# Delta rule's entry: eight extra float32 sums on TensorE, and the gates' products one quarter later

## The chip, the cores and the metric

The kernel runs on one core of a Trainium2 chip, in one launch. The metric is the device time of one execution in microseconds (us). Before the change it is 851.34 us, the median of three runs (849.03 to 851.57). Lower is better.

## The reference

Two transformer blocks in float32 over 256 tokens of width 1024. The first has windowed attention with an mLSTM, cross attention and a gated feed-forward part. The second has a gated delta rule layer and a stick-breaking attention layer. The change lies at the entry of the delta rule:

```python
proj = h @ w_in                                     # q, k, v, z and two gate columns for each of 8 heads
qkv = silu(causal_conv(proj[..., :3 * W], conv_w))  # 4 taps
q = _l2norm(q) * Dh ** -0.5
k = _l2norm(k)                                      # _l2norm: x * rsqrt(sum(x * x) + EPS)
beta = sigmoid(b_raw)
g = -exp(a_log) * softplus(a_raw + dt_bias)         # the gates
o = _chunk_gated_delta(q, k, v, g, beta)            # chunks of 64 tokens, 8 heads of 128
o = _rms(o, o_gain) * silu(z)
y = o @ w_out
```

## The kernel before

Activations lie transposed in on-chip memory, 8 tiles of 128 channels by 256 tokens. Each weight matrix is cut into units of 1024 rows by 256 columns (1 MB). SyncE's queue loads them in a fixed order into five raw buffers. ScalarE (line 1121) writes the rounded high half of a unit and VectorE (line 1522) the low half, in four pieces. A unit is then four "parts" (quarters) on TensorE, each with three products for each of two row blocks: high by high, low activation by high weight, high activation by low weight (line 2047, 12 matmuls in a quarter, 48 in a unit; in this stage the low weight comes last).

A planner in Python (`class Plan`) writes one list of jobs, and each engine carries out its own jobs in the order of that list and waits on counting semaphores. So the list fixes the order on every engine. `step()` adds the next quarter of the weight stream, with pieces of later units' high and low halves ahead of it. `blend()` runs generators beside it: in each round every active generator goes on to its next `yield`, and then one step of the stream is added. A `yield` is so worth a quarter.

In the delta rule's stage two generators are active at a time, first `gdn_gates` and `gdn(0)`:

- `gdn_gates`: g_mm, 32 float32 matmul instructions of 32 columns of weights for the two gates (line 2106), reads the normed activations that ScalarE's job `xa` finishes (line 1179). g_cp copies them (VectorE, line 1732), g_tp adds the four row groups up (TensorE, line 2115). g_abs is exponential and logarithm (ScalarE, lines 1310 to 1317), g_neg, g_a and g_m are VectorE's (lines 1752 to 1772), g_ctp transposes (TensorE, lines 2125 to 2128), then g_col, g_exp and g_c3 (lines 1778, 1322, 1781).
- `gdn(i)`, for a pair of heads: it begins when the SiLU of its pair (`gsilu`, line 1108) and g_c3 stand in the list. d_sq squares q and k (ScalarE, line 1413); d_ones sums over the 128 channels with a matrix of ones (TensorE, line 2246, two float32 matmuls of 512 columns, two instructions each); d_rs is logarithm and exponential (ScalarE, lines 1419 and 1422, behind a table load, line 1100). Then come d_nrm (VectorE, line 1858), d_vtp (line 2252), d_vb (line 1866), d_dec (lines 2261 to 2264, waits for the second d_rs), d_dexp (line 1433), d_ktp (line 2270), d_kt (line 1875), d_kk (line 2278) and the inverse of a triangular matrix in six levels.

The weight stream beside it is unit qkva 0, 4, 8, 1, 5, 9, and so on; the convolution's taps are `gid` (ScalarE, line 1268) and `gtap` (VectorE, line 1519, three instructions for each half of a unit). g_mm stands ahead of the first quarter of qkva 4, g_cp ahead of the second, g_tp, g_abs and g_a ahead of the third, g_m ahead of the fourth; g_ctp and g_col ahead of the third quarter of qkva 8, g_exp and g_c3 ahead of its fourth. d_ones 0 stands behind the third quarter of qkva 1. A `gtap` half stands ahead of each of the first two quarters of a unit. Two older places in the kernel have products that nobody reads: line 2005 at the start, and the job `busy` (line 2073).

Of the kernel before, what the change touches and what calls it, by code (L numbers as in the profile page):

```python
# [14 lines left out]
T = 256  # L15
# [191 lines left out]
class Plan:  # L207
# [23 lines left out]
    def add(self, kind, *i):  # L231
        self.jobs.append((kind, *i))
        self.done.add((kind, *i))
# [159 lines left out]
    def make(self):  # L393
        add = self.add
# [231 lines left out]
        self.handler["za"] = lambda i: add("za", i)  # L626

        def gdn_gates():
            for _ in range(4):
                yield  # L630
            add("g_mm", 2)
            yield
            add("g_cp", 2)
            yield
            add("g_tp", 2)
            add("g_abs", 2)
            add("g_neg")
            add("g_a", 2)
            yield
            add("g_m", 2)  # L640
            for _ in range(3):
                yield
            add("g_ctp", 2)
            add("g_col", 2)
            yield
            add("g_exp")
            add("g_c3")

        def gdn(i):
            while ("gsilu", i) not in self.done or ("g_c3",) not in self.done:  # L650
                yield
            for n in range(2):
                add("d_sq", i, n)
            yield
            for n in range(2):
                add("d_ones", i, n)
                add("d_rs", i, n)
            yield
            for n in range(2):
                add("d_nrm", i, n)  # L660
            add("d_vtp", i)
            add("d_vb", i)
            add("d_dec", i, 0)
            add("d_dexp", i, 0)
            yield
            add("d_dec", i, 1)
            add("d_dexp", i, 1)
            yield
            add("d_ktp", i)
            add("d_kt", i)  # L670
            for n in range(2):
                add("d_kk", i, n)
                add("d_am", i, n)
            add("d_u0", i)
            yield
            add("d_utp", i)
            add("d_t0", i)
            for lev in range(1, 7):
                yield
                add("d_x", i, lev)  # L680
                add("d_xm", i, lev)
                yield
                add("d_uu", i, lev)
                add("d_u", i, lev)
            yield
            add("d_v0", i)
            add("d_v0c", i)
            yield
            add("d_s", i)
            add("d_sc", i)  # L690
            add("d_qd", i)
            add("d_qexp", i)
            add("d_qs", i)
            yield
            add("d_ks", i)
            add("d_vb1", i)
            yield
            add("d_v1", i)
            add("d_v1c", i)
            yield  # L700
            add("d_o", i)
            add("d_osq", i)
            yield
            if i == 3:

                add("d_oz", i)
                for n in range(2):
                    add("d_oones", i, n)
                    add("d_ors", i, n)
                    add("d_on", i, n)  # L710
                yield
                for n in range(2):
                    add("d_ohi", i, n)
                    add("d_olo", i, n)
                return
            add("d_oones", i)
            add("d_ors", i)
            yield
            add("d_on", i)
            while ("za", i) not in self.done:  # L720
                yield "park"
            add("d_oz", i)
            yield "park"
            while ("za!", 3) not in self.done or (i and ("d_ohi", i - 1) not in self.done):
                yield "park"
            add("d_ohi", i)
            yield "park"
            add("d_olo", i)

        self.handler["outa"] = residual("outa", "kv")  # L730
        add("f_m", "kv")
        self.blend([gdn_gates()] + [gdn(i) for i in range(4)], 2, self.at("sbk"))
        self.run_to(self.at("sbk"))
        self.flush_lows()
# [100 lines left out]
def program(nc, xT, memT, cB, vec, con, conr, wg1, wg2, wst, wsd, outT):  # L835
# [11 lines left out]
    with ctx:  # L847
        def sb(name, shape, dt=F32, c=ctx):
            return c.enter_context(nc.sbuf_tensor(name, shape, dt))
# [10 lines left out]
        def on(*job):  # L860
            return S[COUNTED[job[0]]], rank[job]

        def tick(kind):
            return S[COUNTED[kind]], 1
# [15 lines left out]
        ps = [ctx.enter_context(nc.psum_tensor(f"ps{i}", [P, 512], F32))[:, :] for i in range(3)]  # L880
# [6 lines left out]
        cst = sb("cst", [P, NCON])  # L887
# [63 lines left out]
        def C(name, a=0, b=None, p=P):  # L951
            a0, n = CON[name]
            return cst[0:p, a0 + a:a0 + (n if b is None else b)]
# [5 lines left out]
        ident, ones = C("ident"), C("ones")  # L959
# [1033 lines left out]
        def _(t):  # L1993
            e = Once(t)
# [11 lines left out]
            for kind, *i in jobs:  # L2006
                if kind == "part":
                    k, part = i
                    name, n, kc, w = units[k]
                    hi, lo, _ = IN[name]  # L2010
# [20 lines left out]
                    for half in turns:  # L2031
                        a, b = hi if half[0] == "h" else lo, wh if half[1] == "h" else wl
                        for c in chunks:
# [12 lines left out]
                            for q, (o, l, r) in enumerate(ops):  # L2046
                                ins = t.matmul(o, l, r, start=begins and k0 == 0 and half == "hh" and c == 0 and q == 0,  # L2047
                                               stop=ends and not more and half == turns[2] and c == kc - 1 and q == len(ops) - 1,
# [19 lines left out]
                elif kind == "busy":  # L2068

                    name, count = i  # L2070
# [16 lines left out]
                elif kind == "f_ones":  # L2087
# [3 lines left out]
                             stop=True).then_inc(*tick("f_ones"))  # L2091
                elif kind == "f_s1":
                    t.matmul(ps[4][:, 0:T], ones, tr[5][:, 0:T], start=False, stop=True).then_inc(*tick("f_s1"))
                elif kind == "g_mm":
# [7 lines left out]
                    for c in range(KC):  # L2102
                        r = slice(32 * (c % 4), 32 * (c % 4) + 32)
                        for half in range(2):
                            o = (2 * c + half) * n
                            ins = t.matmul(ps[5][r, half * T:(half + 1) * T], g[:, o:o + 32], tmp[:, c, :], start=c < 4 and half == 0,
                                           stop=c >= 4 and half == 1, skip_group_check=True)
# [97 lines left out]
                elif kind == "c_qk":  # L2205
# [6 lines left out]
                    for b in range(2):  # L2212
                        for c in range(2):
                            ins = t.matmul(bank[:, b * T:(b + 1) * T], xq[:, 2 * h + c, b * P:(b + 1) * P], xk[:, 2 * h + c, :],  # L2214
                                           start=c == 0, stop=c == 1)
# [12 lines left out]
                elif kind == "c_av":  # L2228
# [5 lines left out]
                    for c in range(2):  # L2234
                        cc = slice(h * T + c * P, h * T + (c + 1) * P)
                        for m in range(2):
                            ins = t.matmul(ps[4 + 2 * slot][:, c * T:(c + 1) * T], xvv[:, m, cc], pt[:, m * T:(m + 1) * T], start=m == 0, stop=m == 1)  # L2237
                    ins.then_inc(*tick("c_av"))
                elif kind == "d_ones":
                    n_, n = i  # L2240
                    e.wait_ge(*on("d_sq", n_, n))
# [39 lines left out]
                elif kind == "d_utp":  # L2281
                    n_, = i
                    e.wait_ge(*on("d_u0", n_))
                    for h in range(2):
                        for c in range(2):
                            for k in range(2):
                                src = HALVES[k ^ c]
                                ins = t.matmul(xb[n_ % 2][HALVES[k], c, h, :], Uc[n_ % 2][src, c, h, :], ident[src, src],
                                               start=True, stop=True)
# [12 lines left out]
                elif kind == "d_uu":  # L2302
# [3 lines left out]
                    for h in range(2):  # L2306
                        for c in range(2):
                            if lev == 6:
                                ins = t.matmul(ub[n_ % 2][0:64, c, h, :], X_[64:128, c, h, :], Um[n_ % 2][64:128, 2 * h + c, 64:128],
                                               start=True, stop=True)  # L2310
# [24 lines left out]
                elif kind == "d_qd":  # L2335
                    n_, = i
                    for n in range(2):
                        h = 2 * n_ + n
                        ins = t.matmul(ps[4 + 2 * (n_ % 2)][:, n * P:(n + 1) * P], C("ident", h, h + 1, p=8).broadcast_to([8, P]), R2[:, P:T],
                                       start=True, stop=True)  # L2340
# [7 lines left out]
                elif kind == "d_v1":  # L2348
# [3 lines left out]
                    for n in range(2):  # L2352
                        ins = t.matmul(ps[4 + 2 * (n_ % 2)][:, n * P:(n + 1) * P], Um[n_ % 2][:, 2 * n + 1, :], vb[:, 2 * (2 * n_ + n) + 1, :],
                                       start=True, stop=True)
# [151 lines left out]
```

## Time and profile before

| | us |
|---|---|
| median of three runs | 851.34 |
| lowest, highest | 849.03, 851.57 |
| the profiled execution | 849.51 |
| its span, first to last instruction | 847.7 |
| TensorE, VectorE, ScalarE busy in the span | 804.3, 639.5, 494.7 |

The profiled execution is one execution; its mean granted clock of TensorE is 0.994 of full speed. In the rows below a row of an engine's order of time is one run of like instructions: its start, how long it lasted, the line of the kernel and the operands (written tile first). A number in brackets is the time the engine stood idle ahead of it, with the work that ended the wait. TensorE's instructions overlap, so that the steps between starts give the rate and the last one's end is modelled. PE is TensorE, PEld its weight loads (which overlap), DVE VectorE, ACT ScalarE, POOL GpSimd. In the windows the first number behind the stretch is its length, (xN) counts instructions, and a clock of 1.00 is 2.4 GHz, 0.50 is 1.2 GHz.

### The profile page before, as it was taken

What the parts mean: (1) busy time and instruction counts of PE and PEld (TensorE: products, weight loads), DVE (VectorE), ACT (ScalarE), POOL (GpSimd) and SP (SyncE); (2) the same over time, 40 slices, a digit from 0 to 9 for tenths busy, and PEclk for the clock granted to TensorE, in tenths of its full rate; (3) what the DMA queues carried; (4) which work ended last, traced back from release to release, by engine and by line L of the source; (5) the groups of instructions that cost most, each with busy time, mean ns of one, the idle gap of its engine ahead of it and who ended that gap; (6) DMA issues with size and microseconds to landing.
All of it is one profiled execution on the core that took longest, in us unless ns stands there. A gap on an engine that the chain in (4) does not pass through costs nothing.

```text
span 847.7 us, 16950 instructions
## 1 busy us (share of the span) xinstructions
PE 804.3 (95%) x7092; PEld 744.7 (88%) x7092; DVE 639.5 (75%) x1288; ACT 494.7 (58%) x1016; POOL 0.2 (0%) x4
## 2 busy tenths in 40 slices
PE   7999999999999999999998798999999899999988
PEld 5888889999999999999996687888888889978888
DVE  5488988897687899978888777877867778954455
ACT  5578655454456666665547646373756455667762
POOL 0000000000000000000000000000000000000000
PEclk9999999999999999999999899999999999999999
DMA  9632674875455566646793322221324248744211
GB/s 358 240 122 104 237 261 149 288 259 199 158 196 194 193 226 232 230 152 217 272 335 133 100 100 101 101 101 51 116 98 160 82 150 293 293 155 149 100 51 51
DMA packets 22541, 148.52 MB, mean 175 GB/s; under 512 B 2624, under 2 KB 3264, under 8 KB 6336
## 3 DMA queue, kind: packets, MB, share of 16 engines
q1 hardware_dynamic: 22464, 147.43, 49.2%
q8 instruction: 56, 0.92, 0.4%
q14 instruction: 21, 0.17, 0.1%
HBM read 146.37 MB, written 1.05 MB: 174 GB/s over the span
## 4 chain that ended last, share of the span: by engine, by line
PE 72%; DVE 18%; ACT 9%; issue 1%; ACTq 0%; DVEq 0%
PE ps L2047 52%; DVE wlo L1522 4%; DVE raw L1544 3%; DVE tmp L1519 1%; PE pp L2299 1%; PE pp L2319 1%; PE pp L2278 1%; PE pp L2246 1%; PE pp L2237 1%; DVE vt L1519 1%; PE pp L2214 1%; ACT whi L1121 1%; PE pp L2314 1%; PE ps L2005 1%; PE pp L2403 1%
## 5 line engine op out<-in xcount | busy, mean ns | idle before, releaser
L1522 DVE TENSOR_TENSOR wlo<-raw,whi 128x512 fp32r<-128x512 f32 (+2 forms) x436 | 273.8, 659 | 17.0 <-ACT whi L1121 16.6
L1121 ACT ACTIVATE whi<-raw 128x512 fp32r<-128x512 f32 (+2 forms) x436 | 239.1, 600 | 0.0
L2047 PE MATMUL ps<-p0hi,whi 128*128 128x256 f32 x1128 | 192.9, 292 | 6.3 <-ACT p0hi L1173 5.3
L2047 PE MATMUL ps<-p0hi,wlo 128*128 128x256 f32 x1128 | 180.8, 281 | 4.7 <-DVE wlo L1522 4.4
L2047 PE MATMUL ps<-p0lo,whi 128*128 128x256 f32 x1128 | 180.8, 281 | 1.1 <-DVE p0lo L1522 0.9
L2047 PEld LDWEIGHTS ps<-p0hi,whi 128*128 128x128 f32 x1128 | 154.1, 189 | 20.9 <-issue 12.3
L2047 PEld LDWEIGHTS ps<-p0hi,wlo 128*128 128x128 f32 x1128 | 152.9, 189 | 6.6 <-DVE wlo L1522 6.6
L2047 PEld LDWEIGHTS ps<-p0lo,whi 128*128 128x128 f32 x1128 | 153.3, 189 | 2.0 <-DVE p0lo L1522 1.7
L1544 DVE CUSTOM_DVE_ANT_0 raw<-raw,cact,vc 128x1024 f32<-128x1024 f32 x64 | 81.7, 1277 | 0.0
L2047 PE MATMUL ps<-zhi,wlo 128*128 128x256 f32 x176 | 31.1, 280 | 0.6 <-DVE wlo L1522 0.6
L1137 ACT ACTIVATE tr<-x 128x512 f32<-128x512 f32 (+1 forms) x18 | 10.3, 584 | 35.6 <-DVE x L1678 24.1
L2047 PE MATMUL ps<-zhi,whi 128*128 128x256 f32 x176 | 31.0, 279 | 0.0
L2047 PE MATMUL ps<-zlo,whi 128*128 128x256 f32 x176 | 30.8, 278 | 0.0
L1519 DVE SCALAR_TENSOR_TENSOR tr<-pp,tr 128x384 f32<-128x384 f32 x20 | 11.1, 557 | 25.0 <-ACT tr L1502 24.4
L1100 ACT ACT_TABLE_LOAD x22 | 28.2, 1283 | 1.1 <-PEq L2499 0.7
L1693 DVE TENSOR_TENSOR tr<-ps,rs 128x512 f32<-128x512 f32 x22 | 15.1, 688 | 16.5 <-PE ps L2047 16.5
L1228 ACT ACTIVATE tr<-tr,vc 128x256 f32<-128x256 f32 x22 | 13.3, 602 | 22.8 <-DVE tr L1693 22.8
L2047 PEld LDWEIGHTS ps<-zhi,wlo 128*128 128x128 f32 x176 | 25.0, 188 | 1.2 <-DVE wlo L1522 1.2
L2047 PEld LDWEIGHTS ps<-zhi,whi 128*128 128x128 f32 x176 | 25.1, 188 | 0.1
L2047 PEld LDWEIGHTS ps<-zlo,whi 128*128 128x128 f32 x176 | 25.0, 188 | 0.0
L1519 DVE SCALAR_TENSOR_TENSOR Tm<-pp,Tm 128x512 f32<-128x512 f32 (+1 forms) x20 | 12.7, 635 | 13.6 <-PE pp L2319 13.6
L2047 PE MATMUL ps<-q1hi,whi 128*128 128x256 f32 x128 | 21.6, 290 | 0.5 <-ACT q1hi L1170 0.4
(353 smaller groups left out, 1245.3 us busy)
## 6 DMA issues: line engine op xcount, KB each, us to landing
raw<-wst SPq DMA_DIRECT2D x125, 1024.0 KB, 5.0
raw<-wsd SPq DMA_DIRECT2D x16, 704.0 KB, 4.6
x<-xT SPq DMA_DIRECT2D x2, 512.0 KB, 4.6
m_x<-memT SPq DMA_DIRECT2D x1, 1024.0 KB, 8.9
outT<-x SPq DMA_DIRECT2D x3, 256.0 KB, 2.3
cact<-cB SPq DMA_DIRECT2D x1, 512.0 KB, 13.8
cst<-con SPq DMA_DIRECT2D x1, 356.0 KB, 11.8
smo<-conr SPq DMA_DIRECT2D x1, 320.0 KB, 11.4
```

The source lines that it names most:

```text
L1100: act.preload_act_table_set(name)
L1121: act.activation(whi[n % NHL][:, a:b], raw[k % NRAW][:, a:b], ACT.Copy).then_inc(*tick("hi"))
L1137: act.activation(dst, src, ACT.Square).then_inc(*tick("sq"))
L1228: act.activation(tr[c % 3][:, 0:T], tr[3 + c % 3][:, 0:T], ACT.Identity, scale=V("cff_w", c * 3 + 2), bias=V("cff_b", c)).then_inc(*tick(" ...
L1519: return v.scalar_tensor_tensor(out=out, in0=a, scalar=s, in1=b, op0=op0, op1=op1)
L1522: return v.tensor_tensor(lo, src, hi.bitcast(F32), ALU.subtract)
L1544: v.tensor_tensor_reduce(out=r, in0=r, in1=cact[:, :], scale=1.0, scalar=V(bname, 2 * n + m), op0=ALU.mult, op1=ALU.add, accum_out=mod[:, ...
L1693: v.tensor_tensor(tr[3 + c % 3].rearrange("p (m t) -> p m t", m=2), bank_of("up", c).rearrange("p (m t) -> p m t", m=2), rep(rs[:, :], 2), ...
L2005: t.matmul(stats[:, 0:T], tr[3][:, 0:P], tr[3][:, 0:T], start=True, stop=True)
L2047: ins = t.matmul(o, l, r, start=begins and k0 == 0 and half == "hh" and c == 0 and q == 0, stop=ends and not more and half == turns[2] and ...
L2214: ins = t.matmul(bank[:, b * T:(b + 1) * T], xq[:, 2 * h + c, b * P:(b + 1) * P], xk[:, 2 * h + c, :], start=c == 0, stop=c == 1)
L2237: ins = t.matmul(ps[4 + 2 * slot][:, c * T:(c + 1) * T], xvv[:, m, cc], pt[:, m * T:(m + 1) * T], start=m == 0, stop=m == 1)
```

## The change

The generator `gdn_gates` waits five rounds rather than four before g_mm, so that all its jobs stand one quarter later in the list. In `gdn(0)` alone a job `d_busy` of eight stands between the squares and d_ones. On TensorE it waits for g_c3 (which d_ones 0 waits for too) and issues eight float32 matmuls of the matrix of ones with 256 columns of the constants into bank ps[3], which d_ones then overwrites. Nobody reads them. In the new list the quarter of qkva 4 that stood behind g_mm stands ahead of it; g_cp stands behind the second `gtap` half of qkva 0; g_m stands behind `gid` 4; g_ctp is ahead of the fourth quarter of qkva 8 and g_exp, g_c3 behind `gid` 8. The other jobs keep their order.

```diff
--- before.py
+++ after.py
@@ -626,7 +626,7 @@
         self.handler["za"] = lambda i: add("za", i)
 
         def gdn_gates():
-            for _ in range(4):
+            for _ in range(5):
                 yield
             add("g_mm", 2)
             yield
@@ -652,6 +652,8 @@
             for n in range(2):
                 add("d_sq", i, n)
             yield
+            if i == 0:
+                add("d_busy", 8)
             for n in range(2):
                 add("d_ones", i, n)
                 add("d_rs", i, n)
@@ -2236,6 +2238,12 @@
                         for m in range(2):
                             ins = t.matmul(ps[4 + 2 * slot][:, c * T:(c + 1) * T], xvv[:, m, cc], pt[:, m * T:(m + 1) * T], start=m == 0, stop=m == 1)
                     ins.then_inc(*tick("c_av"))
+                elif kind == "d_busy":
+
+                    count, = i
+                    e.wait_ge(*on("g_c3"))
+                    for _ in range(count):
+                        t.matmul(ps[3][:, 0:T], ones, cst[:, 0:T], start=True, stop=True)
                 elif kind == "d_ones":
                     n_, n = i
                     e.wait_ge(*on("d_sq", n_, n))
```

## Rows read from the trace of the kernel before

**Rows 1.** The page, busy time and share of TensorE.

```profile
PE 804.3 (95%) x7092; PEld 744.7 (88%) x7092; DVE 639.5 (75%) x1288; ACT 494.7 (58%) x1016; POOL 0.2 (0%) x4
```

**Rows 2.** Windows: busy PE, PEld, DVE, ACT, POOL, then clock, DMA share, GB/s.

```profile
457.00:458.00 1.00, 0.00 (x0) 0.00 (x0) 1.00 (x4) 1.00 (x4) 0.00 (x0) 1.00 0.00 0
...
481.00:482.00 1.00, 0.00 (x0) 0.00 (x0) 0.94 (x2) 0.62 (x2) 0.00 (x0) 0.93 0.93 393
...
488.00:489.00 1.00, 1.00 (x7) 1.00 (x7) 0.17 (x2) 0.97 (x3) 0.00 (x0) 0.66 0.00 0
...
490.00:495.00 5.00, 5.00 (x31) 3.95 (x30) 4.85 (x12) 2.88 (x11) 0.00 (x0) 1.00 0.43 138
...
673.00:676.00 3.00, 2.81 (x13) 2.52 (x13) 2.89 (x8) 2.42 (x5) 0.00 (x0) 0.50 0.00 0
```

**Rows 3.** TensorE in order of time: start, us, line, operands, [idle before, releaser].

```profile
458.83 1.98 PE L2106 MATMUL pp<-tmp,g 128*32 128x256 f32 x32 [2.18 <-ACT tmp L1179]
...
460.74 0.74 PE L2047 MATMUL ps<-p0hi,whi 128*128 128x256 f32 x4
...
463.91 1.02 PE L2115 MATMUL pp<-tr,cst 128*8 128x512 f32 x2
...
471.33 0.22 PE L2125 MATMUL pp<-cst,rows 8*128 8x8 f32 x1 [0.55 <-DVE rows L1772]
...
471.79 0.74 PE L2047 MATMUL ps<-p0hi,whi 128*128 128x256 f32 x4
...
478.44 0.63 PE L2047 MATMUL ps<-p0hi,wlo 128*128 128x256 f32 x4
...
483.76 3.78 PE L2246 MATMUL pp<-tr,cst 128*128 128x512 f32 x4 [4.69 <-ACT tr L1413]
...
486.55 1.84 PE L2047 MATMUL ps<-p0hi,whi 128*128 128x256 f32 x4
...
489.72 0.36 PE L2261 MATMUL pp<-crt 128*128 128x256 f32 x1
```

**Rows 4.** Chain of waits that ended last: start, us, engine, line.

```profile
483.08 0.64 ACT tr L1413
```

**Rows 5.** VectorE in order of time, 459 to 497 us.

```profile
459.33 2.50 DVE L1522 TENSOR_TENSOR wlo<-raw,whi 128x512 fp32r<-128x512 f32 x4 [0.62 <-ACT whi L1121]
...
463.17 0.68 DVE L1732 COPY tr<-pp 128x512 f32<-128x512 f32 x1
...
463.77 0.68 DVE L1522 TENSOR_TENSOR wlo<-raw,whi 128x512 fp32r<-128x512 f32 x1
...
464.37 1.51 DVE L1519 SCALAR_TENSOR_TENSOR qT<-ps,vc,qT 128x255 f32<-128x255 f32 x3
...
467.24 0.14 DVE L1752 TENSOR_SCALAR sm<-sm 8x1 f32<-8x1 f32 x1 [1.36 <-ACT rows L1317]
...
468.48 0.67 DVE L1522 TENSOR_TENSOR wlo<-raw,whi 128x512 fp32r<-128x512 f32 x1
...
496.02 0.61 DVE L1875 TENSOR_SCALAR tmp<-pp,cols 128x128 f32<-128x128 f32 x2 [0.85 <-PE pp L2270]
```

**Rows 6.** TensorE in order of time, three other places.

```profile
1.18 6.78 PE L2005 MATMUL ps<-tr 128*128 128x256 f32 x16 [1.18 <-DVE tr L1524]
...
448.22 1.46 PE L2073 MATMUL ps<-cst 128*128 128x256 f32 x6
...
672.81 1.08 PE L2047 MATMUL ps<-p0hi,wlo 128*128 128x256 f32 x4 [1.80 <-DVE wlo L1522]
```

**Rows 7.** ScalarE in order of time, 484 to 489 us.

```profile
484.76 1.28 ACT L1100 ACT_TABLE_LOAD   x1
...
486.06 0.69 ACT L1419 ACTIVATE tr<-pp,cst 128x512 f32<-128x512 f32 x1
...
487.58 0.69 ACT L1419 ACTIVATE tr<-pp,cst 128x512 f32<-128x512 f32 x1 [0.17 <-PE pp L2246]
...
488.30 0.63 ACT L1422 ACTIVATE tr<-tr 128x512 f32<-128x512 f32 x1
```

## Prediction

> **What bounds the kernel now.** I read the page first: TensorE is busy for 95% of the span [rows 1]. A stage that leaves TensorE idle is therefore worth a look, and the windows show one. In the microsecond from 481 TensorE does nothing and its granted clock begins to fall from full speed to half (2.4 to 1.2 GHz); it comes back only in the one from 488 [rows 2]. TensorE's own order of time shows why: a quarter of weight unit qkva 1 ends at 479.07, and the first pair's sums of squares (d_ones, line 2246) start at 483.76 after 4.69 us of waiting for ScalarE's squares (line 1413). These four instructions and the next quarter then run at half clock [rows 3].
>
> What releases the squares is read from the chain of waits and VectorE's order. Squares (483.08) wait for the SiLU, the SiLU for the taps of unit qkva 8 (the values' convolution), and VectorE works through taps and low halves almost without a pause from 467.24 to 481.3. It stands idle once ahead of that, 1.36 us before line 1752, for ScalarE's gate work, which came from the gate's selection product g_tp, which came from the copy g_cp [rows 4, 5]. So in this stage VectorE's order bounds the entry of the delta rule, and the gates' chain lies on it. From 490 on TensorE is full again [rows 2].
>
> **The eight sums.** `d_busy` puts eight float32 products of 128x256 on TensorE behind its wait for g_c3, each two instructions. The nearest rows: six such instructions of line 2073 take 1.46 us at full clock, 0.216 us apart, and sixteen of line 2005 take 6.78 us at half clock at the start of the kernel [rows 6]. Sixteen at full clock are 15 x 0.216 + 0.38 = 3.6 us; that and 6.8 are the two bounds. I take 3.6, since TensorE has worked at full clock up to them. They fit in the wait (4.69 now, 5.4 after the shift below), so they cost nothing; the cover fails only if TensorE reaches them less than 3.6 us before the squares land. g_c3 is done before 477 now and some 2 us later after the change, still ahead of them, and nothing behind the added wait starves, because d_ones waits for the same g_c3.
>
> **What a full clock is worth there.** TensorE would win most of 2 us: the quarter behind d_ones would end at about 485.5 + 1.4 rather than 489.3 (486.55 and some 2.7 us at half clock) [rows 3]. But the next product that matters, d_dec (line 2261, at 489.72), waits for the second inverse root, and that is ScalarE's: squares, one high half, a table load of 1.28 us ending at 486.04, then logarithm and exponential twice, ending at 488.93. The first logarithm starts when the table is there, not when the sums are; the second waits 0.17 us for the cold sums [rows 7]. With warm sums the second root ends at 488.76, so d_dec could start at 488.8: a gain of 0.9 us, not 2. The bounds of this gain are 0 (clock falls all the same) and 0.9.
>
> **The gates a quarter later.** This moves g_mm (32 instructions) behind the first quarter of unit qkva 4, and with it g_cp, g_tp, g_abs, g_a, g_m, g_ctp, g_col, g_exp and g_c3 each behind one more quarter of PE, one more high half of ScalarE, and one or two more pieces of VectorE. No DMA is issued with them; SP's and POOL's queues are not passed, but the low halves that free raw buffers shift with VectorE.
> - TensorE waits for `xa` now: 2.18 us, until 458.83. After the change a quarter stands there, which needs the high half of qkva 4; ScalarE makes that right behind `xa`, and it is ready when VectorE's first low half starts, 459.33 [rows 3, 5]. The wait is not filled: 0.5 us longer. A quarter is 1.42 us (14 steps from 471.79 to 478.44, 0.475 each, three to a quarter) and g_mm 1.91 (458.83 to 460.74): first quarter 459.3 to 460.7, g_mm to 462.6, second quarter to 464.1, third to 465.5.
> - VectorE: the copy g_cp starts at 463.17 now, ahead of a low half (0.60) and the second taps (1.42) [rows 5]. After, both come first: g_cp starts at 465.2 and lands 0.74 later (463.17 to g_tp's 463.91), g_tp at 465.95, 2.04 us later than now. TensorE is there at 465.5, so VectorE decides.
> - From g_tp to line 1752 it is 3.33 us (463.91 to 467.24) [rows 3, 5], so line 1752 moves to 469.28. Of the 2.04 us VectorE fills 0.60 with the low half that it does at 468.48 now, the first of those behind g_a. Its idle time grows from 1.36 to 2.8 us: **VectorE is 1.43 us later** from there on. It makes taps and low halves without slack up to the SiLU, so SiLU, squares and d_ones move from 483.76 to 485.2.
> - g_m ends at 473.4 rather than 471.3; TensorE reaches g_ctp at 466.9 + 4 x 1.42 = 472.6 and waits 0.8 there (0.55 now), then some 0.3 for a low half. It gets to d_busy at about 479.8, the sums end at 483.4, and 1.8 us of waiting are left before d_ones at 485.2.
>
> The bounds of this part: 1.43 if nothing absorbs it, and 0 if the taps of this stage were not what the squares wait for, for which no row speaks.
>
> **The sum.** d_dec starts when the second root is there: 488.93 - 0.17 + 1.43 = 490.2, against 489.72 now. That is +0.5 us. Its other waits are shorter. VectorE is 0.9 us later behind its second norm product, but stands idle 0.85 us before d_kt at 496.02 [rows 5], which takes that up; TensorE is full through 490 to 495 [rows 2] and carries 0.5 on, as each engine's order behind it is unchanged. The profiled execution would go from 849.51 (span 847.7 and 1.8 around it) to 850.0. It lies 1.83 under the median of the three runs, 851.34; on that median the sum gives **851.8**.
>
> **A rule on the clock.** The clock doesn't fall at every gap of the size that is left. It stayed full over the 2.18 us before 458.83, and fell after 1.80 us before 672.81, where TensorE then ran at half clock through 673 to 676 [rows 2, 3, 6]. So length alone doesn't decide, and 1.8 us is no safe gap. The Trainium skill, "TensorE: Matmul & The Clock Gate", What's actually happening, says that the monitor's windows run freely and don't start with the kernel; by that rule such a gap is cold in some executions and not in others, here and at 672.81. The trace agrees as far as its two gaps go. By it the sum would be 0.5 in some executions and about 1.4 in others.
>
> **The rivals.**
> 1. *The sums don't keep the clock*: it falls in the 1.8 us that are left. For it: 672.81. Against: 458.83. Then the stage runs as now, 1.43 later: 851.34 + 1.4 = 852.8.
> 2. *Slower than now*: a fall comes late in that gap, so that the cold stretch reaches past d_dec, where TensorE is full. Its price beyond rival 1 is a further stretch like that at 673: 3 us and a part of the next one at half speed, some 1.6 us of TensorE's work [rows 2]. In all 1.43 + 1.6 = 3.0: 854.4. It decides from the point where the half clock still holds at d_dec, 491. Against it: now the stretch ends at 488.3, ahead of d_dec.
> 3. *VectorE's delay is absorbed*, because the gates' chain doesn't move the taps as I read it, and the gain of the clock stands alone: -0.9, 850.4. For it: only that idle times in a trace are inferred. Against it: the 1.36 us before line 1752.
> 4. *The clock elsewhere*, by the rule named above: the stretch at 673 isn't cold. Its 3 us at half clock cost 1.5 us of TensorE's work [rows 2], so 1.5 less: with my sum -1.0 (850.3), with rival 3 -2.4 (848.9).
>
> **How the numbers follow.** My forecast 0.58, rival 1 0.14, rival 2 0.06, rival 3 0.11, rival 4 0.11. All but one lie within 2.5 us of the median, which is the 0.3% that a measurement of this kernel can tell (the three runs alone differ by 2.5). Faster by more than 0.3% is half of rival 4 and a rest: 0.08. Slower is rival 2 and a rest: 0.07. Within 0.3%: 0.85. The range reaches from rival 4's far end (848.9) to rival 1 and half of the step to rival 2: 853.6.
>
> **What would show it.** In the changed kernel's trace: sixteen instructions of the new line end about 1.8 us before d_ones; the granted clock from 481 to 490 is 1.00; g_tp starts near 466, VectorE's idle time before the line that scales -exp(alog) by -1 is 2.8 us rather than 1.4; d_ones near 485.2; the first logarithm follows the table load and not the sums; d_dec near 490.2. The prediction is wrong if g_tp isn't later than 465, if d_ones stays at 483.8, if d_dec comes 1 us or more before 490, or if the sums run at half clock and hold d_ones up.

## The result: slower by half a percent, with the forecast entry intact

The changed kernel takes 854.81 us, the median of 20 executions; the kernel before takes 850.94 in the same 20 turns. The ratio is 1.0052 with a 95% interval of 1.0037 to 1.0066. I had forecast 851.8 and a range up to 853.6, so this is **slower, and above the range**. The single times say more than the median: those of before lie between 849.03 and 852.52, those of the changed kernel between 850.52 and 859.9. Eight of the 20 are over 855. Each execution comes with a mean granted clock of TensorE; it goes from 0.996 in the fastest down to 0.984 in the slowest.

The profiled execution (850.96 us, span 849.2) is one of the quick ones. TensorE's order of time in it, lines 2246 (new) and 2254 (d_ones) among them, columns as in [rows 3]:

```profile
460.12 0.73 PE L2049 MATMUL ps<-p0hi,whi 128*128 128x256 f32 x4 [2.66 <-ACT whi L1123]
...
461.72 1.97 PE L2108 MATMUL pp<-tmp,g 128*32 128x256 f32 x32
...
466.71 1.02 PE L2117 MATMUL pp<-tr,cst 128*8 128x512 f32 x2
...
480.76 3.62 PE L2246 MATMUL pp<-cst 128*128 128x256 f32 x16
485.96 1.98 PE L2254 MATMUL pp<-tr,cst 128*128 128x512 f32 x4 [1.58 <-ACT tr L1415]
...
489.75 0.63 PE L2260 MATMUL pp<-cst,vt 128*128 128x128 f32 x4 [0.41 <-ACT tr L1424]
490.90 0.38 PE L2269 MATMUL pp<-crt 128*128 128x256 f32 x1 [0.52 <-ACT tr L1424]
```

and VectorE's, first low half of the stage and the line that scales -exp(alog), then ScalarE's second load and roots:

```profile
460.10 2.50 DVE L1524 TENSOR_TENSOR wlo<-raw,whi 128x512 fp32r<-128x512 f32 x4 [0.62 <-ACT whi L1123]
...
470.05 0.14 DVE L1754 TENSOR_SCALAR sm<-sm 8x1 f32<-8x1 f32 x1 [2.79 <-ACT rows L1319]
```

```profile
486.96 1.28 ACT L1102 ACT_TABLE_LOAD   x1
488.26 0.69 ACT L1421 ACTIVATE tr<-pp,cst 128x512 f32<-128x512 f32 x1
```

The reader should first subtract 0.77 us: the stage begins that much later (460.10 against 459.33 in [rows 5]). It is lost far ahead of the change: VectorE loses 0.3 us between 20 and 30 us, behind a stretch of TensorE at half clock from 12 to 19, and 0.58 between 405 and 410, where every other profile of this document is later than that of before by the same 0.58. Then every step of the sum is there. g_tp comes 2.03 us later (466.71 against 463.91 in [rows 3]; forecast 2.04). VectorE's idle time is 2.79 (forecast 2.8). d_ones comes at 485.19 on the old scale (forecast 485.2), 1.58 us behind the sums (forecast 1.8), at full clock. The first logarithm follows the table load as in [rows 7]. d_dec comes at 490.13 (forecast 490.2, now 489.72), and the first product of the triangular stage 0.42 us later than before (501.92 less 0.77, against 500.73 in the trace of before). So this quick execution is what the sum described, and the loss must be in the others. The rows with 0.41 and 0.52 in brackets are two waits that the kernel before doesn't have there: it reached both places late and found its operands ready.

### The profile page after: what moved, and what is told of

Its sections match the earlier page's. It is cut to its first block, busy times and chain, and to the rows that moved or that the text cites. A ratio compares the mean times of both kernels' runs of the same rounds, so it can differ in the third digit from the quotient of the medians.

```text
span 849.2 us, 16981 instructions
## 1 busy us (share of the span) xinstructions
PE 807.7 (95%) x7108; PEld 748.8 (88%) x7108; DVE 639.6 (75%) x1288; ACT 494.6 (58%) x1016; POOL 0.2 (0%) x4
## 4 chain that ended last, share of the span: by engine, by line
PE 72%; DVE 17%; ACT 9%; issue 1%; DMA 1%; SPq 0%; ACTq 0%; DVEq 0%
PE ps L2049 54%; DVE wlo L1524 4%; DVE raw L1546 3%; DVE tmp L1521 1%; PE pp L2307 1%; PE pp L2327 1%; PE pp L2286 1%; ACT whi L1123 1%; PE pp L2239 1%; DVE vt L1521 1%; PE pp L2216 1%; PE pp L2322 1%; PE pp L2411 1%; PE pp L2422 1%; DVE kT L1521 1%
## 5 line engine op out<-in xcount | busy, mean ns | idle before, releaser
L1139 ACT ACTIVATE tr<-x 128x512 f32<-128x512 f32 (+1 forms) x18 | 10.2, 583 | 35.6 <-DVE x L1680 24.1
```

Of the source, the lines that this page charges most:

```text
L1139: act.activation(dst, src, ACT.Square).then_inc(*tick("sq"))
```

## Experiments

For each run the time is the median (lowest and highest in brackets), and the ratio is to the executions of the kernel before in the same turns, with its 95% interval. "Sums" are float32 products of a matrix of ones with 256 columns, which nobody reads; each is two instructions. A job `fill` of n issues n of them into a bank that is free there (`stats`, ps[7]); the code cuts show only where it stands in the list, not the lines that issue it. "The wait for `xa`" is TensorE's long wait ahead of g_mm, which with the later gates ends with the high half of qkva 4.

### The changed kernel again

No edit.

> The changed kernel again, for a second profile and its spread. Known: its 20 executions lie between 850.5 and 859.9 with mean granted clocks from 0.984 to 0.996, those of before between 849.0 and 852.5. Theory P (phase): with the certain fall of the clock at the entry gone, the clock's later or earlier changes fall differently in each execution, and a slow execution shows one or more half-clock stretches of about 6.8 us that the profiled one of 850.96 (half clock at 12 to 19 and 674 to 678) doesn't have, anywhere behind 480 us. Theory L (local): a slow execution shows the half clock at the entry itself, from the 1.6 us gap before d_ones on, and nowhere else; then no execution can be over 1.4 + 1.6 above before. P expects a ratio of 1.003 to 1.007 and single executions over 855; L at most 1.0035.

Measured: 856.57 us (852.02 to 857.38), ratio 1.0049 (1.0034 to 1.0064), 8 of 12 executions over 855. Its profiled execution took 857.38, and its windows show the loss:

```profile
491.00:492.00 1.00, 0.96 (x4) 0.77 (x5) 0.98 (x3) 1.00 (x3) 0.00 (x0) 1.00 0.00 0
492.00:493.00 1.00, 1.00 (x7) 0.66 (x6) 1.00 (x4) 0.60 (x3) 0.00 (x0) 0.99 0.06 16
493.00:494.00 1.00, 1.00 (x7) 1.00 (x6) 0.96 (x3) 1.00 (x5) 0.00 (x0) 0.50 0.00 0
...
502.00:503.00 1.00, 1.00 (x7) 1.00 (x7) 0.44 (x1) 0.00 (x0) 0.00 (x0) 0.50 0.00 0
503.00:504.00 1.00, 1.00 (x9) 1.00 (x9) 0.41 (x2) 0.00 (x0) 0.00 (x0) 0.89 0.00 0
```

The granted clock (third number from the right) falls at the very end of the microsecond from 492 and stays at half for 10.2 us in all, with TensorE busy all the time. A second stretch of 3.4 us, from 533.9 to 537.3, lies behind the second pair's d_dec, which waits 0.52 us ahead of it, as it does in the kernel before. In TensorE's order of time it reads so:

```profile
489.89 0.63 PE L2260 MATMUL pp<-cst,vt 128*128 128x128 f32 x4 [0.41 <-ACT tr L1424]
491.04 0.39 PE L2269 MATMUL pp<-crt 128*128 128x256 f32 x1 [0.52 <-ACT tr L1424]
...
493.19 1.05 PE L2049 MATMUL ps<-p0lo,whi 128*128 128x256 f32 x4
...
506.69 0.46 PE L2296 MATMUL pp<-cst,Tm 64*64 64x64 f32 x16 [1.47 <-DVE Tm L1899]
```

From d_ones (486.10) to the first 64x64 product it is 20.59 us, against 16.97 in the trace of before (483.76 to 500.73) and 15.96 in the changed kernel's first profile (485.96 to 501.92): 4.6 us lost behind an entry that had won one. Theory L is out: the fall isn't at the gap before d_ones. Theory P has its stretch behind 480.

### Each part alone

Against the kernel before:

```diff
-            for _ in range(4):
+            for _ in range(5):
                 yield
             add("g_mm", 2)
```

> Only the gates a quarter later; no eight sums. The wait before d_ones is then some 5.3 us, and the clock must fall there as before. Theory P: the fall is certain, so the executions lie as close together as those of before (within 4 us), and their median is 1.4 us above before (1.0017). Rival G (the gates' order is what costs, through later waits of VectorE and TensorE): the spread up to 859 and a ratio of 1.005 are here too, without the sums.

Measured: 853.94 us (851.03 to 856.92), ratio 1.0033 (1.0018 to 1.0047). Both were wrong in part: more than my 1.43, less than all. The profile shows the clock low from 461 to 465, behind the wait ahead of the first quarter of qkva 4:

```profile
458.00:461.00 3.00, 1.03 (x8) 1.04 (x9) 2.37 (x7) 3.00 (x8) 0.00 (x0) 1.00 0.00 0
461.00:464.00 3.00, 3.00 (x30) 1.69 (x32) 2.93 (x7) 2.75 (x6) 0.00 (x0) 0.55 0.18 27
```

From g_mm to g_tp it takes 6.31 us there, 4.99 in the changed kernel's first profile. At the entry it has the old stretch at half clock (6.8 us, from 485.2 to 492.0), and d_dec follows d_ones by 5.85 us, 5.96 in the kernel before: nothing more is lost there.

The other part alone is the changed kernel with `range(4)` again.

> Only the eight sums; gates where they were. 3.6 of the 4.7 us are filled, about 1.1 us of waiting is left. The step of my sum: d_dec 0.9 us earlier, ratio 0.999. Theory P: the fall isn't certain any more, so executions with added half-clock stretches are seen (over 855) and the ratio is 1.002 to 1.006, although the entry itself is shorter. Rival G: ratio 0.999 and executions within 4 us.

Measured: 852.17 us (849.14 to 854.19), ratio 1.0005 (0.9992 to 1.0018). Theory P missed here: no execution over 855, and no loss that can be told. My 0.9 us of gain isn't in the median, but it is in the profile (852.63 us): d_dec follows d_ones by 4.94 us, 5.96 in the kernel before. Two other stretches at half clock hide it there. One of 3.4 us begins at 459.9, behind the old wait of 2.18 us, which [rows 3] shows and [rows 2] shows without a fall: from g_mm to g_tp it takes 6.52 us, 5.08 before. The other, near 675, lasts 6.8 us where the kernel before has 3.4. The two short waits of 0.41 and 0.52 are the same as in the changed kernel, but the clock didn't fall behind them.

### The changed kernel a third time

No edit, one execution.

> The changed kernel a third time, one look: one more draw of where the half-clock stretches lie. Theory P: the entry at full clock, and zero to two stretches of 3.4 or 6.8 us elsewhere behind 480. Theory L: none but at the entry, at about 674 and in the first 20 us.

Measured: 854.51 us. The clock fell at 492 to 496 (3.4 us), and from d_ones to the first 64x64 product it was 17.47 us, 1.5 more than without a fall. So a fall at this place comes with different lengths. The larger part of this execution's excess lies elsewhere: near 677 its half clock lasts 6.8 us rather than 3.4, and VectorE loses 2.3 us between 670 and 700 against the kernel before.

```profile
677.00:683.00 6.00, 4.80 (x22) 4.64 (x22) 4.28 (x8) 2.91 (x6) 0.00 (x0) 0.50 0.41 135
```

### Filling the two short waits, and the long one before d_ones

Against the changed kernel:

```diff
+            if i == 0:
+                add("fill", 1)
             add("d_vtp", i)
             add("d_vb", i)
+            if i == 0:
+                add("fill", 1)
             add("d_dec", i, 0)
```

> The changed kernel with two more float32 sums of 128x256 that nobody reads: one ahead of d_vtp 0 and one ahead of d_dec 0, in TensorE's waits of 0.41 and 0.52 us, into bank ps[7]. Theory W (the sums before d_ones let TensorE run ahead into two short waits, transposes and products of 8 rows, and the clock falls behind them at about 492, where TensorE is the bound): no fall at 492, median 2 to 3 us below the changed kernel's, about 1.002 of before, and no execution over 857. Rival N (the falls are drawn anywhere by chance, not made by those waits): ratio stays at 1.005.

Measured: 852.05 us (850.44 to 854.1), ratio 1.0017 (1.0004 to 1.0029), none of 12 over 855. The same place in its trace:

```profile
490.34 0.59 PE L2256 MATMUL ps<-cst 128*128 128x256 f32 x2
490.90 0.63 PE L2270 MATMUL pp<-cst,vt 128*128 128x128 f32 x4
491.37 0.60 PE L2256 MATMUL ps<-cst 128*128 128x256 f32 x2
492.05 0.38 PE L2279 MATMUL pp<-crt 128*128 128x256 f32 x1
```

```profile
489.00:500.00 11.00, 10.91 (x76) 9.11 (x74) 7.63 (x17) 8.01 (x19) 0.00 (x0) 1.00 0.28 98
```

Neither product waits any more, and the clock stays full from 489 to 500. (It does fall in this profile, for 3.4 us from 460.7, behind the wait for `xa`, which isn't filled here.) d_vtp and d_dec start no earlier against d_ones (4.94 us from d_ones to d_dec with and without the fills), so the two sums bought nothing but the clock.

The counterpart fills the gap that I had suspected, again against the changed kernel:

```diff
-                add("d_busy", 8)
+                add("d_busy", 12)
```

> Twelve sums before d_ones in place of eight: they last until the squares are there, so the 1.6 us wait is gone. If that wait is what lowers the clock (at 492), the median goes down by 2 to 3 us as in the run with two fills. By theory W it doesn't: the waits of 0.41 and 0.52 us lie behind it, so 1.004 to 1.005 and executions over 857 stay.

Measured: 854.1 us (849.96 to 858.92), ratio 1.0042 (1.0024 to 1.006), 4 of 12 over 855. Its profile has no wait before d_ones, the waits of 0.41 and 0.52, and the clock low from 493.9 to 497.3. These two runs went in turns with each other: 2 us lie between their medians, and they differ by which waits are filled. Their intervals just overlap; the profiles and the executions over 855 (none against four) say the same as the medians. **The fall behind d_dec goes away with the two short waits**, and not with the wait that is left before d_ones.

### The long wait ahead of qkva 4

Against the kernel before, so with the later gates and without the eight sums:

```diff
             for _ in range(4):
                 yield
+            add("fill", 6)
+            yield
             add("g_mm", 2)
```

> Gates a quarter later, no sums before d_ones, but six sums in TensorE's wait of 2.66 us ahead of the first quarter of qkva 4. The run with the later gates alone came out 2.7 us above before, 1.3 more than the 1.43 of my sum, and its profile shows a half-clock stretch at 461 to 465. If that fall makes the rest: ratio 1.0017 (1.4 us) here and a spread like that of before. If the rest is later (by VectorE's waits), 1.003 stays.

Measured: 852.33 us (850.52 to 854.57), ratio 1.002 (1.0007 to 1.0033); 0.0017 was forecast. The wait is filled and the clock full in its profile:

```profile
458.00:461.00 3.00, 2.93 (x16) 2.32 (x15) 2.38 (x8) 3.00 (x8) 0.00 (x0) 1.00 0.00 0
461.00:464.00 3.00, 3.00 (x42) 2.05 (x41) 2.93 (x7) 3.00 (x7) 0.00 (x0) 1.00 0.15 27
```

So some 1.1 us of the loss with the later gates alone is this fall (ratios 1.0033 and 1.0020; their intervals overlap, so the size is rough).

The same six sums in the changed kernel, with the short waits left as they are:

> The changed kernel with six sums in its wait of 2.66 us ahead of the first quarter of qkva 4; nothing in the waits of 0.41 and 0.52 us. Two falls were seen in its stage: at about 461, behind that wait, and at about 492. If they add up, this takes some 1 us off the changed kernel (1.003 to 1.004), and executions of 856 and over stay, because 492 stays. If the fall at 461 is what sets off the one at 492, it takes 3 us off like the two fills at d_dec did (1.002).

Measured: 854.02 us (852.53 to 854.9, five executions), ratio 1.0042 (1.0029 to 1.0055). The median fits the first case, the two falls add up; but no execution of 856 was seen, and with five of them that says little. The profile, the median execution, doesn't bear the first case out either: it has no fall behind d_dec.

```profile
490.00:500.00 10.00, 9.48 (x68) 8.19 (x67) 8.08 (x19) 5.78 (x16) 0.00 (x0) 1.00 0.33 107
529.00:532.00 3.00, 3.00 (x18) 2.59 (x16) 2.37 (x6) 1.66 (x5) 0.00 (x0) 0.55 0.28 57
676.00:682.00 6.00, 5.47 (x26) 5.17 (x25) 5.27 (x11) 3.75 (x7) 0.00 (x0) 0.51 0.24 31
```

Its time comes from the other two places: 1.5 us behind the second pair's d_dec and 1.9 us between 670 and 700. Whether the falls at 461 and 492 bear on each other is left open.

### Everything filled, with the gates late and at their old place

Six sums (five with the old place) in the wait for `xa`, twelve (ten) before d_ones, one ahead of d_vtp and one ahead of the pair's first d_dec in the first two pairs. The first run has the gates at their old place.

> Gates where they were in the kernel before; five sums ahead of g_mm, ten before d_ones, one ahead of each of d_vtp and d_dec in the first two pairs. By theory W the clock falls nowhere between 455 and 540: the entry gives its 0.9 us and the falls at 459 and 492 are gone, so 849.5 to 850.5, ratio 0.998 to 0.999. By rival N no better than the sums alone: 1.0005.

Measured: 849.78 us (848.73 to 851.93), ratio 0.999 (0.9978 to 1.0003).

> The gates a quarter later with every wait of the entry filled: six sums ahead of qkva 4, twelve before d_ones, one ahead of d_vtp and of d_dec in the first two pairs. The same fills with the gates at their old place gave 0.999 (849.8). The difference of the two is the price of the later gates without any fall of the clock: 1.43 us by my sum for the entry, so 851.2 and a ratio of 1.0005 to 1.001. If the later gates cost 2.7 us by themselves, as the run without sums gave, 852.5.

> The kernel that came out at 0.999 with the interval 0.9978 to 1.0003, once more: is it under before? By the entry's 0.9 us and no fall under TensorE's work: 0.998 to 0.9995.

Measured in turns with each other: 850.86 us (850.19 to 853.09), ratio 1.001 (0.9998 to 1.0021), with the gates late; 849.39 us (848.87 to 851.85), ratio 0.9996 (0.9986 to 1.0005), at the old place. The difference of the medians is **1.47 us, the 1.43 of my sum**. In all three profiles the clock falls nowhere between 455 and 540. The version with everything filled and the old gates isn't clear of the kernel before in either of its two runs, though both medians lie under it (by 1.2 and 0.75 us), so I don't call it faster.

### The changed kernel a fourth time

No edit, one execution.

> The changed kernel, one more look: whether the clock falls at about 492. So far it did in two of three profiles. If it does, the execution is over 853.5; if not, under it.

Measured: 859.7 us, near the slowest of all. Its windows have the falls one behind the other:

```profile
461.00:464.00 3.00, 2.76 (x12) 2.55 (x12) 2.78 (x5) 3.00 (x8) 0.00 (x0) 0.56 0.00 0
464.00:466.00 2.00, 2.00 (x33) 1.18 (x32) 1.93 (x5) 1.03 (x2) 0.00 (x0) 0.80 0.66 123
...
493.00:496.00 3.00, 2.53 (x13) 2.00 (x14) 2.55 (x7) 2.60 (x8) 0.00 (x0) 0.92 0.02 5
496.00:499.00 3.00, 3.00 (x12) 2.59 (x12) 2.86 (x7) 0.73 (x2) 0.00 (x0) 0.50 0.78 229
499.00:502.00 3.00, 3.00 (x13) 2.35 (x12) 0.23 (x1) 2.07 (x6) 0.00 (x0) 0.50 0.30 123
502.00:505.00 3.00, 3.00 (x16) 3.00 (x16) 0.69 (x3) 0.10 (x1) 0.00 (x0) 0.50 0.00 0
505.00:507.00 2.00, 2.00 (x16) 2.00 (x16) 1.30 (x2) 0.00 (x0) 0.00 (x0) 0.81 0.00 0
```

The second, from 495.5 to 505.7, lies behind d_dec; a third one, at 536 to 540, behind the second pair's d_dec. The first, from 461.4 to 464.8, lies behind this wait:

```profile
461.24 1.14 PE L2049 MATMUL ps<-p0hi,whi 128*128 128x256 f32 x4 [2.67 <-ACT whi L1123]
```

From d_ones to the first 64x64 product it is 20.59 us again. Of the changed kernel's four profiles three have the fall behind d_dec, and these are the three that took 854.5 or more; the one without it took 850.96.

### Where each profiled execution lost its time

VectorE carries out the same number of instructions in every one of these kernels. The table counts them off and gives by how much more time each profile takes for the same stretch of them than the profile of the kernel before, in us; the stretches are named by that kernel's time scale. In brackets stands how long the granted clock was at half in that stretch.

| profile | up to 455 | gates, 455 to 480 | d_ones to past d_dec, 480 to 520 | second pair, 520 to 560 | 560 to 700 |
|---|---|---|---|---|---|
| kernel before | 0 | 0 | 0 (6.8) | 0 | 0 (3.4) |
| changed, first | 0.8 | 1.4 | -1.0 | 0.0 | 0.3 (3.4) |
| changed, second | 0.9 | 1.4 | 3.6 (10.2) | 1.5 (3.4) | 0.4 (3.4) |
| changed, third | 0.6 | 1.4 | 0.5 (3.4) | 0.0 | 2.3 (6.8) |
| changed, fourth | 1.9 | 2.9 (3.4) | 3.6 (10.2) | 1.5 (3.4) | 0.3 (3.4) |
| later gates alone | 0.6 | 3.0 (3.4) | -0.1 (6.8) | 0.0 | -0.1 |
| sums alone | 0.4 | 1.4 (3.4) | -1.0 | 0.0 | 2.3 (6.8) |
| changed, short waits filled | 0.4 | 2.9 (3.4) | -1.0 | 0.0 | 0.4 (3.4) |
| changed, twelve sums | 0.6 | 2.8 (3.4) | 0.6 (3.4) | 0.0 | 2.1 (6.8) |
| later gates alone, `xa` filled | 1.0 | 1.4 | 0.2 (6.8) | 0.0 | 0.1 (3.4) |
| changed, `xa` filled | 0.6 | 1.4 | -1.0 | 1.5 (3.4) | 2.0 (6.8) |
| all filled, gates late | 0.5 | 1.4 | -1.0 | 0.1 | -0.1 |
| all filled, old place | 0.9 | 0.0 | -1.0 | 0.1 | 2.4 (6.8) |
| all filled, old place, again | 0.4 | 0.0 | -1.0 | 0.1 | 0.2 (3.4) |

So each term has its own price in the traces. The later gates cost 1.43. The entry gains 1.0 wherever the sums stand and no fall follows. A fall behind the wait for `xa` costs 1.4 to 1.5, one behind d_dec 1.5 (3.4 us) or 4.6 (10.2 us), one at the second pair 1.5. The last column is common to all kernels, with the change and without: near 675 the half clock lasts 0, 3.4 or 6.8 us, and 6.8 costs some 2 us more than 3.4.

## Why the prediction was wrong

**What held.** That VectorE's order carries the entry, that the later gates cost 1.43 (1.47 measured between two kernels, 2.03 for g_tp against 2.04), that ScalarE's table load caps what a full clock gives at d_dec (1.0 us measured, 0.9 forecast), and that the eight sums themselves hide. The sum's +0.5 is +0.42 in the profile that has no fall. (The sums' other bound, 6.8 us, came from a row at the start of the kernel that was taken for half clock by its step; the granted clock recorded there, from 0 to 8 us, reads 1.00, so no row shows it as half clock.)

**The step that failed** stands in "What a full clock is worth there". It says that TensorE could be ready well ahead of d_dec and that d_dec then waits for the root. That is the same as saying that two waits appear, at d_vtp and at d_dec, where the kernel before has none (d_dec in [rows 3]). I used the new wait as a bound for the gain and did not ask what it does to the clock, although the section on the clock said that length alone doesn't decide a fall. I looked only at the gap of 1.8 us before d_ones. Twelve sums there change little (1.0042), two sums at the short waits take the ratio from 1.0052 and 1.0049 down to 1.0017: some 2.7 to 3 us for this term, which the sum had at nothing. The four profiles agree: 4.6, 1.5, 4.6 and 0 us lost behind d_dec, 2.7 on average.

**A second term was mis-sized**: "The wait is not filled: 0.5 us longer." I let it pass since the clock is full in [rows 2] over the 2.18 us. The runs show that it does fall behind this wait in other executions, with the old order too (459.9 in the profile of the sums alone), and costs 1.4 to 1.5 us when it does. Filling it gave back 1.1 us in the kernel with the later gates alone. How often the kernel before has this fall isn't known, so what the change adds here is open.

**The rivals.** Rival 2 had the mechanism (half clock reaching to where TensorE is full) and nearly the time, 854.4. It had the wrong place, the gap before d_ones, and a chance of 0.06. The argument against it was that the stretch now ends at 488.3. (That was misread: a mean of 0.66 in the microsecond from 488 means half clock until 488.7.) That is the point that I should have turned round: in the kernel before, the half clock from 481.9 to 488.7 lies mostly under a wait and under ScalarE's load, and TensorE comes out of it late and full, with nothing to wait for. The half clock stood where it costs 1.0 us. The sums keep the clock up there, and in three of four profiles it falls some 11 us later, where 10 us of half clock cost 4.6 us. The single executions point the same way: a line through times and clocks gives 0.18 to 0.20 us for each us at half clock in the kernel before (29, 35 and 23 executions), 0.41 in the changed one (20 executions; 0.30 in the repeat of 12), where half the time at half clock is the most that TensorE's work can lose. The mean time at half clock, worked out from the mean granted clocks, is nearly the same, 14.7 and 15.7 us in the same turns: **not more half clock, but half clock in a worse place.**

Rival 1, a fall in the gap that is left before d_ones, is in no profile: wherever the sums stand, the clock is full from 481 to 490. Rival 3, that VectorE's delay is absorbed, is out: the 1.43 us stand in every profile with the later gates. Rival 4 was priced too high. Two profiles have no half clock near 675, and they gain 0.1 to 0.4 us against those with 3.4 us, not 1.5. The other direction, which I had not priced, is the larger one: 6.8 us there cost some 2 us more. That is no part of the change, and the single times of other kernels fit it: the last run of the table has eight of 12 executions at 848.9 to 849.5, three at 851.8 and one between.

The account in us, from ratios times 851: later gates 1.4, the entry's gain -0.3 to -0.9 (the two runs with everything filled), falls behind the wait for `xa` about 1, falls behind d_dec 2.7 to 3. Together 4.2 to 5.1, against 4.4 and 4.2 measured. From the table, as means of the changed kernel's four profiles: 1.43 - 1.0 + 0.4 (`xa`) + 2.7 (d_dec) + 0.7 (second pair) = 4.2. The second pair's falls were seen in three of the seven profiles with the sums and unfilled short waits, and in none of the other seven; no run fills its wait alone, so whether the change makes them is open.

**What stays open.** Why the fall behind d_dec lasts 3.4 us in one execution and 10.2 in others, with TensorE busy throughout. What runs there is transposes, products of 8 rows and of 128 columns among the quarters; no run separates these. The Trainium skill, "TensorE: Matmul & The Clock Gate", Part 4: PE-mode transpose, says that a transpose doesn't count as TensorE's work for the clock in the same way; d_vtp's four lie between the two waits, so the rule fits, but no run here shows it by itself. The transposes aren't enough for a fall: they stand at the same place in the kernel before and with the short waits filled, and the clock doesn't fall behind them there (1.00 from 490 to 495 in [rows 2], and from 489 to 500 above). It is also open why the sums alone lose so little (1.0005) with the same two waits; its 12 executions have 10 us at half clock on average, 15 in the kernel before. The later gates alone have three executions over 855 that weren't profiled; the profile, at 853.12, has no half clock near 675, and 6.8 us there would add 2.0 to 2.4 us by the table and bring it over 855, an estimate.

## What to carry to other kernels

When an edit makes an engine early, write down the waits that it will then have, as new rows, and price them like added work. A low clock under a wait is cheap (6.8 us of it cost 1.0 us here), so before keeping the clock up there, ask where it will fall next and whether the engine is full at that place. And where single executions of the changed kernel spread wider than before's, one profile is one draw: the first profile showed none of the loss that 20 times had shown, and it took three more to find where it lies. Setting each profile against one of the kernel before, instruction count by instruction count, also finds the losses that have nothing to do with the change.

## What the hardware showed that I had not expected

TensorE's clock fell behind two waits of 0.41 and 0.52 us, with four transposes between them and d_dec's products behind them, and stayed at half for 10.2 us under continuous work in two profiles of the same kernel, for 3.4 us in a third, and didn't fall in the fourth. It fell behind a wait of 2.7 us in one of these four profiles and not in the other three. With one sum of 0.43 us in each of the short waits it didn't fall there, in the one profile of that kernel and in the three with everything filled, and none of that kernel's 12 executions was over 855 us.
